# Splitting GpSimd's 128x1024 subtractions into two of 128x512 in a hybrid encoder layer

## The reference

```python
h = _rmsnorm(x, norm1_g)
proj = h @ w_in                                  # 1024 x 2304, split into q, k, v of two head groups
oa = _neighbourhood_attn(qa, ka, va, rpb_a)      # group A: 2-D windows with an offset bias
ob = _windowed_gqa(qb, kb, vb, t5_table, sink_b) # group B: +-128 window, grouped keys
mix = concat([_rmsnorm(oa, outn_a_g), _rmsnorm(ob, outn_b_g)])
x = x + mix @ w_out                              # 1024 x 1024
h = _rmsnorm(x, norm2_g)
x = x + (silu(h @ w_gate) * (h @ w_up)) @ w_down # hidden width 2816
```

## Time and profile before

| what | value |
|---|---|
| median of three runs | 1955.87 us (1954.98 to 1956.47) |
| the profiled execution's own time | 1953.7 us |
| its span, first to last instruction | 1951.9 us |
| PE busy | 1857.9 us (95%) |
| PEld busy | 1671.1 us (86%) |
| DVE busy | 1298.3 us (67%) |
| ACT busy | 1004.0 us (51%) |
| POOL busy | 952.3 us (49%), 807 instructions |
| mean granted TensorE clock | 0.976 |

### The profile page before, as it was taken

One profiled execution on the slowest core, in us unless ns is written; L12 is line 12 of the kernel. 1 busy time (PEld: TensorE's weight loads), 2 busy tenths in 40 slices (PEclk: granted clock), 3 DMA queues, 4 the chain that ended last, 5 costly groups with the idle time before them and its releaser, 6 DMA issues.

```text
span 1951.9 us, 35332 instructions
## 1 busy us (share of the span) xinstructions
PE 1857.9 (95%) x12047; PEld 1671.1 (86%) x12047; DVE 1298.3 (67%) x2349; ACT 1004.0 (51%) x2085; POOL 952.3 (49%) x807
## 2 busy tenths in 40 slices
PE   5999989998998979997999999999999999999998
PEld 3897769998777867886999999899999989999997
DVE  3657658888556885468666666866666676666664
ACT  4555557889346873335534444543534454444432
POOL 1333345765335651114646455555646464655543
PEclk7999998999998989998999999999999999999999
DMA  5444623454222534012423232353233235333221
GB/s 155 151 140 126 171 87 101 112 152 132 79 85 90 164 123 166 33 65 75 132 86 107 86 120 95 102 179 108 92 101 107 86 109 173 109 97 117 86 86 65
DMA packets 184323, 217.10 MB, mean 111 GB/s; under 512 B 13124, under 2 KB 162100, under 8 KB 183964
## 3 DMA queue, kind: packets, MB, share of 16 engines
q1 hardware_dynamic: 184220, 215.77, 35.2%
HBM read 197.34 MB, written 27.27 MB: 115 GB/s over the span
## 4 chain that ended last, share of the span: by engine, by line
PE 56%; DVE 4%; ACT 2%; issue 2%; POOL 2%; DMA 1%; ACTq 0%; SPq 0%; POOLq 0%; DVEq 0%
PE bank L395 19%; PE bank L396 18%; PE bank L397 18%; DVE mvl L2011 1%; POOL msl L1118 1%; ACT msh L1495 0%; DVE tsum L2007 0%; ACT logit L1401 0%; DVE qm L1908 0%; ACT qm L1425 0%; POOL bias L1096 0%; DVE pmeta L1848 0%; DMA draw<-in_w_down 0%; PE bank L2393 0%; ACT pth L1410 0%
## 5 line engine op out<-in xcount | busy, mean ns | idle before, releaser
L395 PE MATMUL bank<-mvh,sth 128*128 128x256 f32 x1848 | 526.5, 285 | 16.4 <-DVE act_f L2027 5.6
L397 PE MATMUL bank<-mvh,stl 128*128 128x256 f32 x1848 | 525.4, 284 | 0.0
L396 PE MATMUL bank<-mvl,sth 128*128 128x256 f32 x1848 | 525.4, 284 | 0.0
L395 PEld LDWEIGHTS bank<-mvh,sth 128*128 128x128 f32 x1848 | 357.0, 193 | 19.5 <-issue 16.0
L396 PEld LDWEIGHTS bank<-mvl,sth 128*128 128x128 f32 x1848 | 357.2, 193 | 1.2
L397 PEld LDWEIGHTS bank<-mvh,stl 128*128 128x128 f32 x1848 | 357.0, 193 | 0.0
L1195 POOL TENSOR_TENSOR dl<-draw,dh 128x1024 fp32r<-128x1024 f32 x66 | 158.1, 2419 | 364.6 <-ACT dh L1588 364.6
L2049 DVE TENSOR_TENSOR y<-bank,y 128x512 f32<-128x512 f32 x264 | 182.4, 692 | 162.6 <-PE bank L397 161.6
L1055 POOL TENSOR_TENSOR wl<-wraw,wh 128x1024 fp32r<-128x1024 f32 x54 | 131.3, 2432 | 252.3 <-ACT wh L1246 252.3
L1189 POOL TENSOR_TENSOR stl<-graw,sth 128x512 fp32r<-128x512 f32 x132 | 177.6, 1346 | 101.2 <-ACT sth L1570 97.1
L395 PE MATMUL bank<-dh,acth 128*128 128x512 f32 x528 | 208.9, 396 | 7.7 <-DVE y L2049 5.3
(11 more groups left out here) (247 smaller groups left out, 4267.5 us busy)
## 6 DMA issues: line engine op xcount, KB each, us to landing
graw<-in_w_gate SPq DMA_DIRECT2D x33, 1024.0 KB, 5.4
uraw<-in_w_up SPq DMA_DIRECT2D x33, 1024.0 KB, 5.4
draw<-in_w_down SPq DMA_DIRECT2D x66, 512.0 KB, 4.2
wraw<-in_w_in SPq DMA_DIRECT2D x54, 512.0 KB, 4.0
bias_rows<-table_a SPq DMA_DIRECT2D x36, 192.0 KB, 3.1
out<-y SPq DMA_DIRECT2D x12, 512.0 KB, 3.2
bias<-table_b SPq DMA_DIRECT2D x28, 201.0 KB, 2.6
table_a<-line_a_dram SPq DMA_DIRECT2D x8, 576.0 KB
```

Source lines behind the costliest of these rows:

```text
L395: pe.matmul(out, lhs[0], rhs[0], start=start, stop=False, skip_group_check=True)
L396: pe.matmul(out, lhs[0], rhs[1], start=False, stop=False, skip_group_check=True)
L397: return pe.matmul(out, lhs[1], rhs[0], start=False, stop=stop, skip_group_check=True)
```

## The change

Each 128x1024 subtraction on POOL becomes two of 128x512, the first and the second half of the free dimension, in the same place of POOL's list. The wait stands ahead of the first half and the semaphore is raised by the second. Nothing else is edited; the 132 instructions (54, 12 and 66) become 264.

```diff
             def weight_lo(G):
                 pool.wait_ge(w_hi, G + 1)
-                pool.tensor_tensor(wl[G % 2][:, :, :], wraw[G % 2][:, :, :], f32(wh[G % 2][:, :, :]),
-                                   ALU.subtract).then_inc(w_lo, 1)
+                for part in (slice(0, 4), slice(4, 8)):
+                    op = pool.tensor_tensor(wl[G % 2][:, part, :], wraw[G % 2][:, part, :],
+                                            f32(wh[G % 2][:, part, :]), ALU.subtract)
+                op.then_inc(w_lo, 1)
 ...
             def mix_lo(i, slot):
                 waits_apart(pool, (ms_hi, i * 2 + slot + 1))
-                pool.tensor_tensor(msl[slot][:, :, :], mix_tile(i, slot), f32(msh[slot][:, :, :]),
-                                   ALU.subtract).then_inc(ms_lo, 1)
+                for part in (slice(0, 4), slice(4, 8)):
+                    op = pool.tensor_tensor(msl[slot][:, part, :], mix_tile(i, slot)[:, part, :],
+                                            f32(msh[slot][:, part, :]), ALU.subtract)
+                op.then_inc(ms_lo, 1)
 ...
             def down_low(c):
                 for j in range(2):
                     pool.wait_ge(down_hi, c * 2 + j + 1)
-                    pool.tensor_tensor(dl[j][:, :], draw[j][:, :], f32(dh[j][:, :]), ALU.subtract).then_inc(down_lo, 1)
+                    for part in (slice(0, 512), slice(512, 1024)):
+                        op = pool.tensor_tensor(dl[j][:, part], draw[j][:, part], f32(dh[j][:, part]), ALU.subtract)
+                    op.then_inc(down_lo, 1)
```

## The result

The changed kernel takes 1960.48 us in the median of seven runs, against 1955.87 us before, also of seven (+4.6 us); the ratio is 1.0026 with an interval of 1.0015 to 1.0037. The profiled execution took 1959.6 us, its span is 1957.8 us, 5.9 us longer than the one before.

The account below looks back on a forecast made before the run. The prediction took PE, busy 95% of the span, as the bound. Its terms 0.9 + 0.3 + 0 + 2.3 + 2.0 + 0 = 5.5 us on 1955.9 gave 1961.4 us, range 1957.0 to 1963.3.

Parts of the forecast that it names:

- mix loop, six `msl`: Mix loop: each of the six `msl` on the chain costs its split of 0.15 us in full, +0.9 us.
- projections, `wl`: Projections: PE comes 0.15 us later in each of segments 1 and 2, delays not adding, +0.3 us together.
- feed-forward, `dl` and `stl`: Feed-forward cycles: `stl` of up comes 0.3 us later behind two `dl`, but PE's running work hides it, 0.
- `scale_pair` behind the halves: At 720 to 731 us: `scale_pair` ends 2.3 us later, and the last `w_out` blocks with it, +2.3 us.
- longer half clock: Behind the `w_out` blocks: PE's clock rises only after restarting in one go, past `osum`; +2.0 us.
- `htl` at the sample's projection: At 484.78 us: `htl` gets its turn earlier, PE's last blocks gain 0 to 1.0 us; taken as 0, range -1.0 to +0.5.
- The turns: At 720 us: POOL and DVE alternate by whole instructions, so a split `msl` gives DVE a turn between its halves.
- the forecast's chain of 1.09 and 1.14 us: 720 to 731 us: DVE ends 1.09 us after POOL, a 512-wide POOL instruction 1.14 after DVE; `scale_pair` ends at 730.65.
- One of the two rows that gave the range: Clock term: half clock after PE restarts, 188.1 to 191.5 and 884.4 to 891.2 us; half lost, 1.7 to 3.4 us.
- The rival of the early rise: Clock behind 720 us: `scale_pair` 2.3 us late, PE loses at most a few tenths to the clock; 1959.4 us, chance 0.20.
- The faster rival: `w_out` blocks and segment 2's start: earlier `wol` and `htl` set PE's pace; 1953.9 or 1951.7 us, chance 0.05.
- the forecast's own range: Whole time: 1960.0 to 1963.2 us, from a clock term of 0.6 to 3.4 us and the 484 us term; chance 0.55.

Follow-up runs that it names:

- e5: The changed kernel with the last `scale_pair` moved up in POOL's queue, from behind the four `msl` halves to between the second and third; ratio 1.0008.
- e6: The kernel before with only the first two `msl` cut, each in four of 128x256; executed once, 1962.15 us, no ratio.
- e11: The changed kernel with no further edit, measured once more (the table's "again"); 1960.43 against 1955.56 us, ratio 1.0026.
- e1: The kernel before with only the `msl` made as halves, `wl` and `dl` whole; ratio 1.0017.
- e12: The same kernel as e1 with no edit, measured once more; ratio 1.0026.
- e7: The kernel before, differences whole, `scale_pair` ahead of the second `msl`, which waits until DVE has made all eight `wol`; 1953.40 us, ratio 0.9987.

## Why the prediction was right

1960.48 us lies within 0.9 us of the forecast of 1961.4, and the profiled execution (1959.6) within 0.4 of the 1959.2 that the sum gave. Step by step:

| step | forecast | measured (changed, again) |
|---|---|---|
| mix loop, six `msl` | +0.9 | +0.88, +0.82 |
| projections, `wl` | +0.3 | +0.12, +0.15 (segment 2; segment 1 not told apart from 0) |
| feed-forward, `dl` and `stl` | 0 | 0 |
| `scale_pair` behind the halves | +2.3 | +2.26, +2.23 |
| longer half clock | +2.0 (0 to 3.4) | +2.32, +2.18 |
| `htl` at the sample's projection | 0 (-1.0 to +0.5) | -0.64, -0.63 |
| sum | 5.5 | 4.9, 4.8 |

- **The turns** are shown, not only argued: halves of `msl` ended 1.26, 3.47, 5.70 and 7.92 us after the first one's start (1.28, 3.51, 5.74 and 7.97 by the forecast's chain of 1.09 and 1.14 us), `scale_pair` 10.15 (10.20). e5 and e6 say the same with another order and another size.
- **The clock** was the weakest term, half of a range. Its size came out within 0.3 us, but not by the forecast's way, so part of it is luck. The forecast had PE at half clock up to one late rise, once it had restarted in one go. In the changed kernel the clock had risen at 726.3 already and fallen at 729.8, while PE paused. The other three profiles with a term of 2.1 to 2.5 us had likewise risen ahead of `osum` and fallen again (e11 at 2.4 GHz from 727.5 to 737.7, e6 from 728.8 to 735.7, e1 in two stretches from 727.9 to 738.2). In e12 PE also paused up to `osum` at half clock, yet the clock rose right there and the term was 0.13; in e5 it had risen and fallen, and rose again 0.9 us behind `osum` (+0.36). So pausing up to `osum` doesn't decide it, and what does stays open. One of the two rows that gave the range was misread: at 884.4 us PE was busy 5.61 of 6.80 us, no restart in one go. The rival of the early rise was no idle one: its price is what the profile of e12 shows.
- **Projections:** half of the term is there. In segment 2 PE comes 0.12 and 0.15 us later, the forecast's 0.15. In segment 1 single half-steps start 0.14 us later (at 164.4 and 171.2 us of the trace before, against the matmuls ahead), but by 185 us no more than 0.05 us of it is left in the changed kernel and in e11; a half-clock stretch behind that hides what the end of the segment keeps.
- **The `htl` term** was taken at the wrong place within its bounds. The last `htl` ends 0.55 us earlier (493.41 instead of 494.81 in the two traces, less the 0.85 us that the changed one was ahead by), and PE's work after it gains 0.64. I feared that gaps in PE's first blocks would keep the clock low and give it back; PE has those gaps, but in the changed profile the clock is at 1.00 there, and in those of e5 and e11 it is at 0.50 with the same gain. What ends last is DVE's row, not PE; its last two `htl` wait 1.17 us for POOL's `qm`, so not all of the 1.0 us that the first two `htl` gain arrives. DVE's rows, before and then changed:

```profile
488.93 5.88 DVE L1758 TENSOR_TENSOR htl<-qm,hth 128x512 fp32r<-128x512 f32 x6
```
```profile
492.12 1.29 DVE L1764 TENSOR_TENSOR htl<-qm,hth 128x512 fp32r<-128x512 f32 x2 [1.17 <-POOL qm L1115]
```

- **The faster rival** (the shorter wait wins) had this piece right, and at 720 us early blocks did come earlier: counted from the first `msl`'s start, PE began the second and third block 1.8 and 2.2 us earlier than before. They didn't count, because the last two blocks hang on `scale_pair`, and PE began the seventh 2.1 us later; e5 shows that this loss goes if `scale_pair` goes ahead.
- **Agreement by cancelling:** the missed -0.64 us is most of the difference between 5.5 and 4.9. In the one profile the columns that scatter add 1.1 us (-0.85 + 0.23 + 1.71), so that its 5.9 us fits 5.5 better than it should. And the forecast's own range leaves the `htl` term out at its lower end: with -1.0 us it reaches down to 1959.0, not 1960.0.

The rule of the Trainium skill that the prediction named ("SBUF — State Buffer", section "SBUF: two separate sides") is borne out by the turns: 2.25 to 2.30 us for an instruction that takes 1.27 alone. The gain that it alone would suggest, the shorter wait, is there at the sample's projection. At 720 us the same lock costs more than it gives, as it hands out turns per instruction and the more urgent instruction stood in the longer queue.

## What to carry to other kernels

Where two engines take turns at a port, an instruction is a turn: cutting one that both compete over in two lets the other engine in once more, if that has an instruction waiting, and everything queued behind the pieces comes later by such a turn. So look first at what stands behind the pieces in that queue, and move what gates a transfer ahead of what is needed late: that took back the whole loss at 720 us (e5). Holding an instruction that is needed late out of the other engine's way as well gained 2.4 us over the kernel before (e7). And cutting an instruction in the middle of a chain paid here only where the consumer was let go by the first piece: with one signal at the end the halves cost 0.9 us in the mix loop, with a signal each they gained 3.3 us.

## What the runs showed of the hardware

- A pause of PE costs more than the timeline shows between two matmuls: with 0.24 us shown, the next product started 0.48 us later than without the pause, and closing six of them gained 3.3 us, not the 1.6 that the brackets add up to.
- The granted clock is no fixed consequence of a program: after the same pause of 2.64 us at about 1231 us it fell to half in ten of fourteen profiles, and stayed at 2.4 GHz in four. Such a fall cost 1.4 to 1.6 us. Two traces of the same kernel, e1 and e12, differ by 2.4 us in the stretch behind `osum`, by when the clock rose there. Single runs of the kernel before lie between 1950.2 and 1962.3 us; an effect of one or two us is found in a stretch of the trace, not in the whole time.
